# A recurrent unit in a streamed fp32 kernel: inner gates, powers and gate fills put in another order

## The reference

```python
def recurrent_mixer(xn, w_in, conv_w, conv_b, gate_a_w, gate_a_b, gate_x_w, gate_x_b, lam, w_out):
    gate_branch, rec_branch = jnp.split(xn @ w_in, 2, axis=-1)      # 2 x 1280 channels
    gate = jax.nn.gelu(gate_branch, approximate=True)
    rec = causal_depthwise_conv(rec_branch, conv_w) + conv_b        # 4 taps
    h = rg_lru(rec, gate_a_w, gate_a_b, gate_x_w, gate_x_b, lam)
    return (gate * h) @ w_out

def rg_lru(xs, wa, ba, wx, bx, lam):                                # 10 blocks of 128 channels
    r = sigmoid(xb @ wa + ba); i = sigmoid(xb @ wx + bx)            # "inner gates"
    log_a = 8.0 * r * log_sigmoid(lam)
    a = exp(log_a)
    b = sqrt(-expm1(2.0 * log_a)) * (i * xs)
    h[t] = a[t] * h[t - 1] + b[t]                                   # a scan over the tokens
```

## Time and profile before

| what | value |
|---|---|
| median of 3 runs | 2289.04 us (2288.18 to 2289.15) |
| the profiled execution, its own time | 2286.85 us |
| its span, first to last instruction | 2285.1 us |
| mean granted TensorE clock | 0.971 of full speed |
| PE busy over the span | 94% |
| DVE busy | 67% |
| ACT busy | 53% |
| the recurrent stage, on PE | 1378.16 to about 1496 us |

### The profile page before, as it was taken

The page is one execution under the profiler, slowest core; times in us unless marked ns, Lnnn a source line. Parts: engine busy times, 40 slices in busy tenths (PEclk is TensorE's granted clock), DMA queues, the critical chain, the costliest instruction groups (busy, mean ns, idle before and its releaser), DMA issues.

```text
span 2285.1 us, 29090 instructions
## 1 busy us (share of the span) xinstructions
PE 2152.0 (94%) x10942; PEld 1808.3 (79%) x10942; DVE 1531.0 (67%) x2045; ACT 1211.9 (53%) x1606; POOL 50.8 (2%) x71
## 2 busy tenths in 40 slices
PE   5599999997999999999899999699988999999999
PEld 5378887886978888777898889688875788898887
DVE  8987568887567558888766557755555555576554
ACT  4145457775455446777445445754445544445443
POOL 5300000000000000000000000000000000000000
PEclk9799999999999999999899999899998999999999
DMA  5145669996514558999456654465532366555662
GB/s 209 56 139 187 198 223 331 353 348 255 185 57 164 187 193 290 350 366 332 146 168 211 190 186 131 143 190 191 187 127 83 112 202 193 186 175 174 197 192 101
DMA packets 123004, 451.58 MB, mean 198 GB/s; under 512 B 13808, under 2 KB 13808, under 8 KB 121968
## 3 DMA queue, kind: packets, MB, share of 16 engines
q1 hardware_dynamic: 121536, 442.03, 56.9%
q0 software_dynamic: 1040, 6.82, 0.8%
q10 hardware_dynamic: 288, 0.88, 0.1%
HBM read 448.62 MB, written 1.05 MB: 197 GB/s over the span
## 4 chain that ended last, share of the span: by engine, by line
PE 81%; DVE 10%; ACT 4%; DMA 3%; issue 2%; SPq 0%; ACTq 0%; DVEq 0%
PE bank L303 21%; PE bank L305 21%; PE bank L304 21%; DVE w_lo L279 4%; PE bank L296 3%; PE bank L297 3%; PE bank L298 3%; DMA raw<-in_stream 3%; ACT w_hi L272 1%; DVE scr L2578 1%; DVE scr L2563 1%; PE bank L649 1%; PE bank L420 1%; PE bank L1089 1%; PE bank L2029 1%
## 5 line engine op out<-in xcount | busy, mean ns | idle before, releaser
L279 DVE TENSOR_TENSOR w_lo<-raw,w_hi 128x1024 fp32r<-128x1024 f32 x829 | 989.9, 1222 | 517.6 <-ACT w_hi L272 511.3
L272 ACT ACTIVATE w_hi<-raw 128x1024 fp32r<-128x1024 f32 x839 | 875.5, 1058 | 679.0 <-PE bank L305 538.9
L303 PE MATMUL bank<-w_hi,x_hi 128*128 128x512 f32 (+1 forms) x1056 | 413.5, 392 | 1.0 <-DVE x_lo L547 1.0
L305 PE MATMUL bank<-w_hi,x_lo 128*128 128x512 f32 (+1 forms) x1056 | 410.9, 389 | 0.0
L304 PE MATMUL bank<-w_lo,x_hi 128*128 128x512 f32 (+1 forms) x1056 | 410.5, 389 | 0.0
L303 PE MATMUL bank<-w_hi,c_hi 128*128 128x512 f32 x906 | 358.7, 396 | 39.4 <-issue 19.4
L304 PE MATMUL bank<-w_lo,c_hi 128*128 128x512 f32 x906 | 356.2, 393 | 0.0
L305 PE MATMUL bank<-w_hi,c_lo 128*128 128x512 f32 x906 | 355.8, 393 | 0.0
L303 PEld LDWEIGHTS bank<-w_hi,c_hi 128*128 128x128 f32 x906 | 172.2, 190 | 80.6 <-issue 32.0
L303 PEld LDWEIGHTS bank<-w_hi,x_hi 128*128 128x128 f32 x1056 | 199.2, 189 | 41.0 <-DVE x_lo L547 1.3
L305 PEld LDWEIGHTS bank<-w_hi,x_lo 128*128 128x128 f32 x1056 | 198.9, 188 | 41.0
(11 more groups left out here) (393 smaller groups left out, 1989.1 us busy)
## 6 DMA issues: line engine op xcount, KB each, us to landing
raw<-in_stream SPq DMA_DIRECT2D x839, 512.0 KB, 4.4
ln_rows<-in_ln POOLq DMA_DIRECT2D x4, 1024.0 KB, 5.4
scr<-in_xt SPq DMA_DIRECT2D x1, 1024.0 KB, 5.1
scr<-in_s POOLq DMA_DIRECT2D x1, 1024.0 KB, 10.7
x<-in_x POOLq DMA_DIRECT2D x1, 1024.0 KB, 5.2
out_x<-x SPq DMA_DIRECT2D x4, 256.0 KB, 2.7
par<-in_par ACTq DMA_DIRECT2D x1, 830.0 KB, 10.6
ln_rows<-in_ple POOLq DMA_DIRECT2D x1, 512.0 KB, 12.5
```

Source lines behind the costliest of these rows:

```text
L272: nc.scalar.activation(w_hi[:, n % RING, :], raw[:, n % RING, :], ACT.Copy).then_inc(hi_done, 1)
L279: nc.vector.tensor_tensor(w_lo[:, n % RING, :], raw[:, n % RING, :], w_hi[:, n % RING, :].bitcast(F32), ALU.subtract).then_inc(lo_done, 1)
L303: nc.tensor.matmul(out, xh, hi, start=start, stop=False)
L305: return nc.tensor.matmul(out, xl, hi, start=False, stop=stop)
```

## The change

The weights of the stage come in another order, PE multiplies the inner gates of pair g after the rec fill of pair g + 2 (or a gate fill, for the last pairs), and the three last gate fills stand after all inner gates. rstd is spread after the first half of rec fill 1. "log a" is no longer formed by DVE: ACT applies the decay as scale and bias of exp, exp and tanh, which makes these operations one per chunk (256 columns) where it was one per pair (512 columns). They stand in the same loop as the inner gates. All five gelus come after the square roots. The table with exp and tanh is loaded ahead of the first tap. The setup, in the stage before, has one small DVE instruction more (twice the decay). The banks of inner gates and gate fills are others.

```diff
-        decay = norm[:, 44:44 + LC]
+        decay, twice_decay = norm[:, 44:44 + LC], small[:, 2 * LC:3 * LC]
         def lru_gate_bank(g):
-            return psum[5 + g if g < 3 else g - 1]
+            return psum[(1, 2, 3, 0, 1)[g]]
         def lru_inner_bank(g, j):
-            return psum[(2 * g + j) % 8]
+            return psum[(5, 6)[j] if g % 2 == 0 else (7, 0)[j]]
         def lru_pe(pe, st):
-            for g in range(LG):
-                fill("rec", g, psum[g], g == 0)
-                if g == 0:
-                    spread_pe(pe, st, psum[7])
-            for g in range(3):
-                fill("gate", g, lru_gate_bank(g))
-            for g in range(LG):
+            def inner(g):
                 pe.wait_ge(dve_did["inner lo"], dve_did.at("inner lo", st, g))
...
-            for g in range(3, LG):
+
+            fill("rec", 0, psum[0], first=True)
+            fill("rec", 1, psum[1], between=lambda: spread_pe(pe, st, psum[7]))
+            fill("rec", 2, psum[2])
+            inner(0)
+            fill("rec", 3, psum[3])
+            inner(1)
+            fill("rec", 4, psum[4])
+            inner(2)
+            fill("gate", 0, lru_gate_bank(0))
+            inner(3)
+            fill("gate", 1, lru_gate_bank(1))
+            inner(4)
+            for g in (2, 3, 4):
                 fill("gate", g, lru_gate_bank(g))
             outer_pe(pe, st, range(LC), 0, LC - 1)
...
+            def powers(g):
+                act.wait_ge(act_did["r"], act_did.at("r", st, g))
+                act.wait_ge(dve_did["input gated"], dve_did.at("input gated", st, g))
+                for c in (2 * g, 2 * g + 1):
+                    d, d2 = decay[:, c:c + 1], twice_decay[:, c:c + 1]
+                    nc.scalar.activation(lru_a[:, c, :], lru_r[:, c, :], ACT.Exp, bias=d, scale=d)
+                    last = nc.scalar.activation(lru_x[:, c, :], lru_r[:, c, :], ACT.Exp, bias=d2, scale=d2)
+                link(act, "act", last)
+                for c in (2 * g, 2 * g + 1):
+                    d = decay[:, c:c + 1]
+                    last = nc.scalar.activation(lru_r[:, c, :], lru_r[:, c, :], ACT.Tanh, bias=d, scale=d)
+                last.then_inc(act_did["a"], act_did.next("a", st, g))
...
+            split_hi(act)
+            rms_act(act, st)
+            split_hi(act, 1)
+            nc.scalar.preload_act_table_set("exp_and_others")
+            first_tap(0)
+            split_hi(act, 1)
+            inner_hi(0)
+            first_tap(1)
+            split_hi(act)
+            inner_hi(1)
+            first_tap(2)
+            split_hi(act)
+            inner_gates(0)
+            inner_hi(2)
+            first_tap(3)
+            split_hi(act)
+            inner_gates(1)
+            inner_hi(3)
+            first_tap(4)
+            powers(0)
+            split_hi(act)
+            inner_hi(4)
+            inner_gates(2)
+            powers(1)
+            split_hi(act)
+            inner_gates(3)
+            powers(2)
+            split_hi(act)
+            inner_gates(4)
+            powers(3)
+            split_hi(act, 1)
+            powers(4)
+            split_hi(act, 1)
             for g in range(LG):
                 act.wait_ge(dve_did["minus b2"], dve_did.at("minus b2", st, g))
                 nc.scalar.activation(pair(lru_x, g), pair(lru_x, g), ACT.Sqrt, scale=-1.0).then_inc(
                     act_did["root"], act_did.next("root", st, g))
+            split_hi(act, 1)
+            for g in range(4):
+                gelu(g)
+            gated_hi(0)
             split_hi(act)
-            for g in range(3, LG):
-                gelu(g)
+            gated_hi(1)
+            gelu(4)
+            split_hi(act)
+            gated_hi(2)
...
-                nc.vector.scalar_tensor_tensor(pair(lru_r, g), pair(lru_r, g), 1.0, over_tokens(decay[:, 2 * g:2 * g + 2]), ALU.add, ALU.mult).then_inc(
-                    dve_did["log a"], dve_did.next("log a", st, g))
...
+            spread_dve(dve, st, psum[7])
+            rec(0)
+            split_lo(dve, 1)
+            taps(0)
+            rec(1)
+            split_lo(dve, 1)
+            inner_lo(0)
+            taps(1)
+            rec(2)
+            split_lo(dve)
+            inner_lo(1)
+            taps(2)
+            rec(3)
+            split_lo(dve)
+            gate_input(0)
+            inner_lo(2)
+            taps(3)
+            rec(4)
+            split_lo(dve)
+            gate_input(1)
+            inner_lo(3)
+            taps(4)
+            minus_b2(0)
+            split_lo(dve)
+            inner_lo(4)
+            gate(0)
+            gate_input(2)
+            minus_b2(1)
+            split_lo(dve)
+            gate_input(3)
+            gate(1)
+            minus_b2(2)
+            split_lo(dve)
+            gate_input(4)
+            minus_b2(3)
+            split_lo(dve, 1)
+            gate(2)
+            minus_b2(4)
+            split_lo(dve, 1)
+            v(nc.vector.memset(lru_a[:, :, 0:1], 0.0))
+            gate(3)
+            split_lo(dve, 1)
+            scan(0)
+            scan(1)
+            gated_lo(0)
+            gate(4)
+            split_lo(dve)
+            scan(2)
+            gated_lo(1)
+            split_lo(dve)
+            scan(3)
+            gated_lo(2)
...
```

More of the change, by code:

```diff
@@ L105 @@
             "k", "v copy", "magnitude", "softplus", "weights", "conv c", "conv h", "conv b", "conv out",
-            "rec", "convolved", "gated", "inner lo", "gate", "half bias", "log a", "minus b2",
+            "rec", "convolved", "gated", "inner lo", "gate", "half bias", "input gated", "minus b2",
             "latent", "latent variance", "latent lo", "angle", "head variance", "normed", "rope",
@@ L321, in signal_product, with product @@
                 last.then_inc(pe_did["tile"], pe_did.next("tile", tile=tile))
-        def product(pe, n_out, ks, xh, xl, out, fill, ready=None):
+        def product(pe, n_out, ks, xh, xl, out, fill, ready=None, claim=True):
             for n in range(n_out):
@@ L1720, in lru_act, with first_tap @@
         def lru_act(act, st):
-            split_hi(act)
-            rms_act(act, st)
-            for g in range(LG):
+            def first_tap(g):
                 act.wait_ge(dve_did["rec"], dve_did.at("rec", st, g))
@@ L1732, in lru_act, with inner_gates @@
                     act_did["inner hi"], act_did.next("inner hi", st, g))
[L1733 to L1738, removed]
-                gelu(g)
-            act.wait_ge(dve_did["half bias"], dve_did.at("half bias", st))
-            for g in range(LG):
+            def inner_gates(g):
+                if g == 0:
+                    act.wait_ge(dve_did["half bias"], dve_did.at("half bias", st))
                 for j, (name, dst) in enumerate((("r", lru_r), ("i", lru_i))):
@@ new lines, in gelu, with gated_hi @@
+            def gelu(g):
+                act.wait_ge(dve_did["gate"], dve_did.at("gate", st, g))
+                nc.scalar.activation(pair(lru_gate, g), pair(lru_gate, g), ACT.Gelu_apprx_tanh).then_inc(
+                    act_did["gelu"], act_did.next("gelu", st, g))
+            def gated_hi(g):
+                round_c(act, st, g, pair(lru_x, g), "dve", ("gated", st, g))
+            split_hi(act)
+            rms_act(act, st)
+            split_hi(act, 1)
+            nc.scalar.preload_act_table_set("exp_and_others")
@@ L1761, in lru_act @@
                     act_did["root"], act_did.next("root", st, g))
+            split_hi(act, 1)
+            for g in range(4):
+                gelu(g)
+            gated_hi(0)
             split_hi(act)
-            for g in range(3, LG):
[L1764 to L1768, removed]
+            gated_hi(1)
+            gelu(4)
+            split_hi(act)
+            gated_hi(2)
+            split_hi(act)
+            gated_hi(3)
+            split_hi(act, 1)
+            gated_hi(4)
             split_hi(act, lead_of(st + 1) - act_at.tile)
@@ L1793, in v, with rec @@
                 link(dve, "dve", ins)
[L1795 to L1804, removed]
+            def rec(g):
                 dve.wait_ge(pe_did["rec"], pe_did.at("rec", st, g))
@@ L1807, in lru_dve, with taps @@
                     dve_did["rec"], dve_did.next("rec", st, g))
+            def taps(g):
                 dve.wait_ge(dve_did["rec"], dve_did.at("rec", st, g))
-                if g:
-                    split_lo(dve)
-                    inner_lo(g - 1)
                 dve.wait_ge(act_did["inner hi"], act_did.at("inner hi", st, "first tap", g))
@@ L1819, in lru_dve, with inner_lo @@
                 last.then_inc(dve_did["convolved"], dve_did.next("convolved", st, g))
-                dve.wait_ge(dve_did["convolved"], dve_did.at("convolved", st, g))
+            def inner_lo(g):
+                dve.wait_ge(act_did["inner hi"], act_did.at("inner hi", st, g))
+                nc.vector.tensor_tensor(pair(c_lo, g), pair(lru_x, g), pair(c_hi, g).bitcast(F32), ALU.subtract).then_inc(
```

(30 more changed lines are left out.)

18 lines of the change are left out of this document (12 added, 6 removed).

## The result

| | median | runs | profiled execution, its span |
|---|---|---|---|
| before, the three runs shown above | 2289.04 us | 2288.18 to 2289.15 | 2286.85, 2285.1 |
| before, six runs (with three beside the changed kernel) | 2284.80 us | 2276.86 to 2289.15 | |
| after, six runs | 2268.22 us | 2264.99 to 2270.94 | 2269.69, 2267.9 |

The ratio of after to before is 0.9928, with a 95% interval of 0.9915 to 0.9941: 16.5 us faster, 13.5 to 19.4. My 2275.5 was 7.3 us too high and the range, 2271.5 to 2280, does not hold 2268.2. The direction was right, and my gain of 13.5 us (ratio 0.9941) stands at the edge of the interval.

A forecast was written before the change was run, and what follows sets the result against it. The recurrent stage was taken as bound by a chain through ACT, then DVE's scans. Out product 13.9 us earlier, less 0.4 for clock and DVE, gives 13.5; 2289.04 - 13.5 = 2275.5 us, range 2271.5 to 2280.

The forecast's parts named there:

- ACT's 28.0 us chain: ACT, from `inner_hi(4)` through gates, powers, splits and roots to split 22, takes 28.0 us without idle time.
- the powers at 3.1: ACT's six 256-column operations per pair, with scale and bias from SBUF columns, cost 3.1 us a pair.
- DVE's 7.0 us behind it: After ACT's chain, DVE's `w_lo` 22, scan(0), scan(1) and `gated_lo(0)` take 7.0 us before the out product.
- the late tiles: Weight tiles 18, 20, 21 and 22 reach PE late by 0.7, 0.7, 1.1 and 2.0 us, covered by slack.
- The 0.4 for the clock and DVE: In the out product, a charge of 0.4 us for a longer low clock and DVE barely keeping up.
- I take the same gain off the median: For the whole kernel's time, the 13.5 us gain is subtracted from the median 2289.04, giving 2275.5 us.
- only lengthens PE's wait later: In the rec loop, PE's 5 us from the earlier spread would only add to its later wait.
- B: Rival: tiles 1 us later each starve PE in the gate fills, the clock falls; gain 9 to 11, 2279; chance 0.10.
- My sign of being wrong: In the changed profile, the clock falling in the gate fills was one listed sign that the forecast was wrong.
- C: Rival: tanh and exp want different tables, seven loads in ACT's chain, 9.0 us less gain, 2284.5; chance 0.04.
- D: Rival: hand-overs pace the rec loop, PE loses 3.6 us five times, 18 us; 2291 at 10.8; chance 0.03.
- E: Rival: the next stage takes the gained time back, 2288 us or so; chance 0.03.

The follow-up runs named there:

- before's second profile: The kernel before, unedited, timed and profiled again: ratio 1.0010 to before, median 2283.4 us, out product at 87.3 us, stage 118.5 us.
- the repeat: The changed kernel, unedited, timed and profiled again: median 2268.57 us, ratio 0.9947 to before, out product at 74.6 us, stage 106.1 us.
- Spread first: The changed kernel with the rstd spread back between rec fills 0 and 1: ratio 0.9941 to before, out product at 77.5 us, stage 109.7 us.
- more PE: The changed kernel with every inner-gate product made twice: ratio 0.9951 to before, out product at 77.4 us, stage 108.9 us.

## Why the prediction was right in the stage and wrong in the time

*Sum.* The gain was put together as 13.9 - 0.4. The start of the out product moved by 14.1 us against 13.9; that it came so close is in part luck, for against before's second profile it moved by 12.7. Of the steps under it, ACT's 28.0 us chain, the powers at 3.1, DVE's 7.0 us behind it and the late tiles (0.35, 0.41, 0.90 and 1.84 us, laid out as 0.7, 0.7, 1.1 and 2.0) came as worked out. The 0.4 for the clock and DVE had the wrong sign: the out product and the closing step took 30.1 us from its start against 30.8 before, since the clock was low for 3.4 us of it and not for the first 4.8; so 14.8 in all in these two profiles. In before's second profile the clock was at 0.50 behind the first gap for some 3 us where the earlier trace rows has 6.1, that length was 30.0 and the stage 118.5, so the same change is worth 12.5 to 14.8 us by how long the clock stays low after the gaps of the kernel before. 13.5 lies between.

*What failed* is the step that is not about the stage: "that execution stands 2.2 us under the median (0.1%), and I take the same gain off the median: 2289.04 - 13.5". I took three runs within 1 us of each other for the level of the kernel, a term of the sum for which I allowed no error. Its runs spread from 2275.7 to 2292.0, with medians of 2282.7, 2284.8, 2283.7 and 2283.3 over 17, 16, 11 and 9 runs. From 2283, 13.5 off gives 2269.5, 1.3 us above the measured median. Of the 7.3 us by which I was off, 4.2 are this level (2289.04 against 2284.80 over six runs) and the other 3.1 the gain as timed, 16.6 between the medians against 13.5, at the edge of its interval; the repeat timed it at 12.1 (14.1 between its medians). The same range set around 2284.80 would be 2267.3 to 2275.8 and hold the result. Why the first three runs stood together at 2289 is not known. The bounds of the range came from costs inside the stage alone and none stood for the level.

*A step that was wrong without being seen in the time*: that PE's 5 us from the earlier spread "only lengthens PE's wait later". Spread first and more PE show that rec fill 4 reaches DVE just as DVE is ready for it: with the 2.8 us of the gap taken away again the chain was 2.9 us longer. What the part of the 5 us that stood for the low clock is worth was not seen, since the clock stayed high in that run. My own schedule had the coincidence (rec 4 done at 1410.55, DVE ready at 1410.45, 0.3 us of waiting charged) and I did not read it as a shared path.

*Rivals.* B: the tiles came no later than laid out. The clock stayed at 1.00 in the gate fills of the first profile, with waits up to 1.84 us, but fell behind the wait of 1.84 us in the repeat, as shown above; since it fell for the last 12 matmuls only, PE's slack covered it. My sign of being wrong, a fall of the clock in the gate fills, so came in one of two profiles without moving the out product (74.6 in both). C, D and E did not come: one table; no rec or inner product is waited for in a way that PE shows; the next stage has PE busy for 103.42 of 104 us as before.

## What to carry to other kernels

When an edit lays PE's work under another engine's chain, follow every engine's order in turn, and where two arrive within a few tenths of a us, count both as the path: the slack of either is zero. An earlier start is only worth what the engines behind it can follow; here two edits that started the out product earlier gained nothing, since DVE had its splits to do. Do not count on the clock to come out the same behind a gap: look at more than one profile. And set the range of an absolute time by the spread of the kernel's own runs, not by three that agree.

## What the runs showed of the hardware that I had not expected

The granted clock of the same kernel, in a stage that the change leaves alone, was 0.50 in one execution and 1.00 in another over the same 20.5 us, with PE busy for 20.5 and 19.5 of them; the mean over the span was 0.974 and 0.977. What decides it was not tried. Nor does one gap give one clock: behind the gap of 2.8 us at the spread the clock was low for the whole 6.1 us of the earlier trace rows in the first profile of before, for about half of that in the second, where it is 1.00 again from 1390.0, and not at all in spread first.

```profile
1386.60:1389.80 3.20, 2.85 (x13) 2.88 (x14) 1.28 (x4) 0.37 (x1) 0.00 (x0) 0.50 0.69 221
```

The line is of before's second profile. A wait of 1.84 us was followed by 1.00 in one profile of the changed kernel and by 0.50 in the other.

One thing that I did expect came out: a scale and a bias from columns of SBUF make a 256-column activation cost 0.59 to 0.61 us, about as long as a 512-column one without them (0.62). The Trainium skill ("ScalarE: Activation LUTs", What ACT_TABLE_LOAD costs) puts each such operand at about 93 ns and a column at 0.833 ns. By these figures, as an estimate, 256 columns fewer take off 0.213 us and two operands add 0.186; the trace agrees.
